# Rotary keys of the paged cache gathered straight into SBUF by GpSimd, instead of through a DRAM copy and ScalarE's loads

## What is computed

```python
# page_table (8, 32) int32: physical page of each of the 32 pages of a decode row
# cache_mla_latent (pages, 128, 256), cache_mla_krope (pages, 128, 32)
c_all  = concat([cache_mla_latent[page_table].reshape(b, 4096, 256), c], axis=1)
kr_all = concat([cache_mla_krope[page_table].reshape(b, 4096, 32), kr], axis=1)
s = (einsum('bqhc,bsc->bhqs', q_lat, c_all) + einsum('bqhr,bsr->bhqs', q_pe, kr_all)) * MLA_SCALE
p = masked_softmax(s)
o_lat = einsum('bhqs,bsc->bqhc', p, c_all)
```

## Time and profile before

| | |
|---|---|
| three runs | 736.41, 732.91, 735.43 us, median 735.43 |
| the profiled execution | 736.41 us, its span 734.6 us |
| tensor engine (PE) busy | 687.2 us, 94% |
| VectorE (DVE) / ScalarE (ACT) / GpSimd (POOL) busy | 439.2 / 212.3 / 64.2 us |
| moved by DMA | 178.60 MB, mean 243 GB/s |

### The profile page before, as it was taken

The page is one execution under the profiler, slowest core; times in us unless marked ns, Lnnn a source line. Parts: engine busy times, 40 slices in busy tenths (PEclk is TensorE's granted clock), DMA queues, the critical chain, the costliest instruction groups (busy, mean ns, idle before and its releaser), DMA issues.

```text
span 734.6 us, 14345 instructions
## 1 busy us (share of the span) xinstructions
PE 687.2 (94%) x5297; PEld 441.2 (60%) x5297; DVE 439.2 (60%) x1231; ACT 212.3 (29%) x579; POOL 64.2 (9%) x68
## 2 busy tenths in 40 slices
PE   9997999999979988789999999969999999999996
PEld 3443444544446655466776666547778888885452
DVE  3296799568647765675565555443577666644244
ACT  0302215545324443343334443221111111110111
POOL 0343341030000000202102000000000000000000
PEclk9999999989989999999999999999999999999999
DMA  9999994987879999996776788995110303026011
GB/s 342 412 415 421 417 397 174 369 306 311 307 214 339 355 375 326 378 364 232 233 247 219 264 288 251 328 366 234 58 57 1 115 1 115 1 103 271 29 50 39
DMA packets 64736, 178.60 MB, mean 243 GB/s; under 512 B 7225, under 2 KB 15698, under 8 KB 57370
## 3 DMA queue, kind: packets, MB, share of 16 engines
q1 hardware_dynamic: 47640, 124.88, 47.7%
q0 software_dynamic: 7840, 48.38, 16.6%
q10 hardware_dynamic: 9186, 4.42, 2.5%
HBM read 169.12 MB, written 12.72 MB: 248 GB/s over the span
## 4 chain that ended last, share of the span: by engine, by line
PE 67%; DMA 15%; SPq 6%; DVE 5%; issue 4%; ACT 2%; ACTq 0%; DVEq 0%
PE bank L1423 18%; PE bank L855 8%; PE bank L1463 8%; PE bank L1266 6%; DMA ring<-latent 6%; DMA W<-w_attn 4%; SPq L627 4%; PE bank L1018 3%; PE bank L1153 3%; PE bank L1250 3%; DMA projP<-x 2%; PE bank L1235 2%; PE bank L1132 2%; PE bank L1455 2%; PE bank L1140 2%
## 5 line engine op out<-in xcount | busy, mean ns | idle before, releaser
L855 PE MATMUL bank<-W,XG 128*128 128x494 f32 x192 | 85.2, 589 | 4.4 <-DMA W<-w_attn 3.9
L1484 ACT ACTIVATE projP<-bank 128x128 f32<-128x128 f32 (+5 forms) x87 | 33.6, 391 | 96.2 <-PE bank L1423 47.5
L2452 DVE TENSOR_TENSOR projP<-projP,bank 128x260 f32<-128x260 f32 x83 | 33.9, 423 | 45.1 <-PE bank L1423 44.3
L855 PEld LDWEIGHTS bank<-W,XG 128*128 128x128 f32 x192 | 35.8, 195 | 41.3 <-issue 40.0
L1266 PE MATMUL bank<-W 128*128 128x260 f32 x256 | 60.4, 389 | 0.0
L1484 ACT ACTIVATE W<-bank 128x512 f32<-128x512 f32 (+2 forms) x69 | 39.8, 582 | 66.6 <-PE bank L898 18.9
L1682 ACT ACTIVATE projP<-bank,projP 128x128 f32<-128x128 f32 (+3 forms) x96 | 49.8, 524 | 29.6 <-DVE projP L2154 29.1
L1266 PEld LDWEIGHTS bank<-W 128*128 128x128 f32 x256 | 47.3, 190 | 10.4 <-issue 3.2
L2154 DVE CUSTOM_DVE_ANT_0 bank<-bank,maskb 128x128 f32<-128x128 f32 (+3 forms) x96 | 45.8, 510 | 12.7 <-PE bank L1132 12.0
L1463 PE MATMUL bank<-ring,W 128*128 128x512 f32 x112 | 49.6, 594 | 1.4 <-issue 1.4
L1132 PE MATMUL bank<-W 64*128 64x128 f32 (+7 forms) x192 | 46.8, 471 | 1.0 <-ACT projP L1682 0.6
(11 more groups left out here) (436 smaller groups left out, 1119.8 us busy)
## 6 DMA issues: line engine op xcount, KB each, us to landing
ring<-latent SPq DMA_DIRECT2D x200, 256.0 KB, 6.7
XG<-latent SPq DMA_DIRECT2D x56, 256.0 KB
W<-w_gate SPq DMA_DIRECT2D x12, 1024.0 KB, 4.8
W<-w_attn SPq DMA_DIRECT2D x16, 494.0 KB, 9.9
rope_pages<-ring SPq DMA_DIRECT2D x2, 2048.0 KB, 10.3
KRR<-rope_pages ACTq DMA_DIRECT2D x32, 128.0 KB
ring<-w_out SPq DMA_DIRECT2D x2, 2048.0 KB, 13.2
o_win<-win SPq DMA_DIRECT2D x1, 4088.0 KB
```

Source lines behind the costliest of these rows:

```text
L855: mm = pe.matmul(bank[2 * (u % 2) + n][:, 0:GW], XG[:, k * TOK + tl * P:k * TOK + (tl + 1) * P], w_part(half, k, n), start=(k == 0), stop= ...
L1484: return act.activation(dst, src, ACT.Copy, scale=scale)
```

## The change

The changed kernel does without `rope_pages`, the two 2 MB gathers, the two stores and ScalarE's 32 loads. GpSimd gathers the rows of each pair straight from `krT` into `KRR`, by four gathers of 128 rows of 512 bytes (64 KB). Their row numbers are 64 more columns of `idxi`, made from a third copy of the page table (`pt4`) by four more small matmuls and one more VectorE instruction at the start, with a new table `exp4` of 128 columns among the first constants. The gathers of pair 0 stand behind GpSimd's memsets and wait for `pooled`; those of pair p wait for `ds` of pair p - 1. The 16 gathers of the selected branch (slc), which were the end of GpSimd's list, now stand between them, four each behind the gathers of pairs 7 to 10. SP's `o_win` and latent jobs no longer wait for `rope_out`. Two shared semaphores (`cst_in`, `x_again`) are split by what their waiters need.

```diff
+    put("exp4", (np.arange(4)[:, None] == p[None] // 32).astype(np.float32))
...
-            for half in range(2):
-                sp.wait_ge(S["rope_in"], 16 * (half + 1))
-                sp.dma_start(rope_pages.rearrange("(p h) n -> p h n", h=2)[:, half], slot[0]).then_inc(S["rope_out"], 16)
...
-            sp.wait_ge(S["rope_out"], 32)
             for m in range(3):
                 latents(m)
...
-            pool.wait_ge(S["pt_in"], 64)
-            pool.wait_ge(S["summed"], N_GATHERS)
-            gather(slot[0], rope_cache, pti[:, 320:321], S["rope_in"])
-            pool.wait_ge(S["rope_out"], 16)
-            gather(slot[0], rope_cache, pti[:, 321:322], S["rope_in"])
...
-            pool.wait_ge(S["idxs"], 1)
-            for r in range(4):
-                n = J_SLC + r
-                slot_free(pool, n)
+            pool.wait_ge(S["pooled"], 8)
+            mla = [c for c in chunks if c["kind"] == "mla"]
+            for p2 in range(16):
+                if p2:
+                    pool.wait_ge(S["ds"], mla[p2 - 1]["q"] + 1)
                 for j in range(4):
-                    gather(job(n)[:, j * 1024:(j + 1) * 1024], t["slc"], idxi[:, 32 + 4 * r + j:33 + 4 * r + j], S[slot_sem(n)])
+                    gather(KRR[:, j * P:(j + 1) * P], t["krT"], 32 + 4 * p2 + j, S["kr_landed"])
+                if 7 <= p2 < 11:
+                    n = J_SLC + p2 - 7
+                    pool.wait_ge(S["idxs"], 1)
+                    slot_free(pool, n)
+                    for j in range(4):
+                        gather(job(n)[:, j * 1024:(j + 1) * 1024], t["slc"], 96 + 4 * (p2 - 7) + j, S[slot_sem(n)])
...
+                for i2 in range(2):
+                    for jl in range(2):
+                        mm = pe.matmul(bank[7][64 * i2:64 * i2 + 64, 32:96].rearrange("p (a h l) -> p l a h", h=2, l=2)[:, jl], C("exp4", 64 * jl, 64, rows=4),
+                                       ptf[0:4, 32:96].rearrange("p (a i h) -> p i a h", i=2, h=2)[:, i2], start=True, stop=True)
...
-                    pe.wait_ge(S["kr_landed"], 32 * (p2 + 1))
+                    pe.wait_ge(S["kr_landed"], 64 * (p2 + 1))
...
-            rope_rows(0)
             act.wait_ge(S["prep_dve"], 1)
...
-                    c = SOFT_at[d]
-                    dec_exp(c)
-                    if c["kind"] == "mla" and c["no"] < 15:
-                        rope_rows(c["no"] + 1)
+                    dec_exp(SOFT_at[d])
...
+            ts(idxi[:, 32:96], bank[7][:, 32:96], 32.0, ALU.mult, C("mod", 1, 1), ALU.add).then_inc(S["idx"], 1)
```

More of the change, by code:

```diff
@@ L198, in build @@
         maskb = sb("maskb", SEQ, BF16)
-        idxi = sb("idxi", 32 + 16, I32)
-        pti = sb("pti", 32 + 32 + 256 + 2, I32)
+        idxi = sb("idxi", 32 + 64 + 16, I32)
+        pti = sb("pti", 32 + 64 + 32 + 256, I32)
         sm = sb("sm", SMALL)
-        rope_cache = t["krT"].rearrange("(a d) c -> a (d c)", d=ROPE_D)
-        rope_pages = nc.dram_tensor("rope_pages", (2 * P, 32 * P), F32, kind="Internal").ap()
         bank = [ctx.enter_context(nc.psum_tensor(f"bank{i}", [P, 512], F32)) for i in range(8)]
@@ L692, in _ @@
             slot_free(sp, J_X)
-            sp.dma_start(job(J_X).rearrange("p (t c) -> p t c", t=TILES), t["x"][0:SEQ].rearrange("(t p) c -> p t c", p=P)).then_inc(S["x_again"], 16)
+            sp.dma_start(job(J_X).rearrange("p (t c) -> p t c", t=TILES), t["x"][0:SEQ].rearrange("(t p) c -> p t c", p=P)).then_inc(S["xend_in"], 16)
             sp.wait_ge(S["z_ps"], z_at[tile_no["pa", 7], 1])
-            sp.dma_start(OA[0:DEC, 0:D_MODEL], t["x"][SEQ:TOK]).then_inc(S["x_again"], 16)
-            sp.dma_start(OB[:, 0:D_MODEL], t["norm_post"].broadcast_to([P, D_MODEL])).then_inc(S["x_again"], 16)
+            sp.dma_start(OA[0:DEC, 0:D_MODEL], t["x"][SEQ:TOK]).then_inc(S["xend_in"], 16)
+            sp.dma_start(OB[:, 0:D_MODEL], t["norm_post"].broadcast_to([P, D_MODEL])).then_inc(S["xend_in"], 16)
             for i, tl in enumerate(WO):
@@ L713, in _, with gather @@
             pool.dma_start(petile[0:CMP_BLOCK], t["pe"]).then_inc(S["pe_in"], 16)
-            def gather(dst, src, rows, sem):
+            def gather(dst, src, col, sem):
                 pool.indirect_dma_start(out=dst, out_offset=None, in_=src,
-                                        in_offset=bass.IndirectOffsetOnAxis(ap=rows, axis=0)).then_inc(sem, 16)
-            pool.wait_ge(S["idx"], 1)
+                                        in_offset=bass.IndirectOffsetOnAxis(ap=idxi[:, col:col + 1], axis=0)).then_inc(sem, 16)
+            pool.wait_ge(S["idx"], 2)
             pool.wait_ge(S["w_in7"], 16)
@@ L725, in _ @@
                     pool.wait_ge(S["summed"], g - N_HALVES + 1)
-                gather(half_slot(g), t["cmp"], idxi[:, g:g + 1], S[f"half{g % N_HALVES}"])
-            pool.wait_ge(S["pt_in"], 64)
-            pool.wait_ge(S["summed"], N_GATHERS)
-            gather(slot[0], rope_cache, pti[:, 320:321], S["rope_in"])
-            pool.wait_ge(S["rope_out"], 16)
-            gather(slot[0], rope_cache, pti[:, 321:322], S["rope_in"])
+                gather(half_slot(g), t["cmp"], g, S[f"half{g % N_HALVES}"])
             tiles_evicted(pool, 8)
@@ L818, in pages @@
                 pe.wait_ge(S["cst_first"], 16)
-                pe.wait_ge(S["ptf"], 2)
-                pe.matmul(bank[7][:, 0:32], C("exp8", rows=8), ptf[0:8, 0:32], start=True, stop=True).then_inc(S["prep_ps"], 1)
+                pe.wait_ge(S["ptf"], 3)
+                pe.matmul(bank[7][:, 0:32], C("exp8", rows=8), ptf[0:8, 0:32], start=True, stop=True)
+                for i2 in range(2):
+                    for jl in range(2):
+                        mm = pe.matmul(bank[7][64 * i2:64 * i2 + 64, 32:96].rearrange("p (a h l) -> p l a h", h=2, l=2)[:, jl], C("exp4", 64 * jl, 64, rows=4),
+                                       ptf[0:4, 32:96].rearrange("p (a i h) -> p i a h", i=2, h=2)[:, i2], start=True, stop=True)
+                mm.then_inc(S["prep_ps"], 1)
                 pe.wait_ge(S["pe_in"], 16)
@@ L1622, in _ @@
             copy(VV[:, :].rearrange("p (t c) -> p t c", t=TILES), pP[:, :, C_VS:C_KC]).then_inc(S["prep_by_act"], 1)
-            mla = [c for c in chunks if c["kind"] == "mla"]
-            def rope_rows(p2):
-                if p2:
-                    act.wait_ge(S["ds"], mla[p2 - 1]["q"] + 1)
-                else:
-                    act.wait_ge(S["pooled"], 8)
-                    act.wait_ge(S["rope_out"], 32)
-                for i2 in range(2):
-                    src = rope_pages[16 * p2 + 8 * i2:16 * p2 + 8 * i2 + 8].rearrange("(j q) (d c) -> (q d) j c", q=2, d=32)
-                    act.dma_start(KRR[64 * i2:64 * i2 + 64, 0:512].rearrange("p (j c) -> p j c", j=4), src).then_inc(S["kr_landed"], 16)
             for i, h in enumerate(HQ):
@@ L2143, in _ @@
             dve.wait_ge(S["prep_ps"], PREP_PS["idxs"])
-            ts(idxi[:, 32:48], bank[5][:, 16:32], C("mod", 2, 1), ALU.add).then_inc(S["idxs"], 1)
+            ts(idxi[:, 96:112], bank[5][:, 16:32], C("mod", 2, 1), ALU.add).then_inc(S["idxs"], 1)
             settle()
```

31 lines of the change are left out of this document (16 added, 15 removed).

## The result

In the measurement made beside the prediction the changed kernel took 752.1 us (749.96 to 753.76, four runs; three more executions on record took 751 to 757), the kernel before 734.2 us. The ratio is 1.027, with a 95% interval of 1.021 to 1.032: slower, by 18 us, where the forecast was 7 us faster. The forecast's upper end, 735.0, is missed by 17 us.

A forecast was written before the change was run, and what follows sets the result against it. It took the tensor engine (94% of the span) as the bound, with transfers bounding the attention from latents(4) to 300 us. -5.0 - 2.0 + 0.3 = -6.7 us, from the median 735.43, gave 728.7 us; range 725.0 to 735.0.

The forecast's parts named there:

- The wait of 5.0 us: At the first pair, the tensor engine's wait for KRR, 204.29 to 209.33 us, goes: -5.0 us.
- the clock's 2.0: At the first pair, without the wait, work from 209.33 to 214.85 us runs at the full clock: -2.0 us.
- the prediction's 186 to 208: Time in us when the last KRR row of pair 0 is there, 208 being the far end.
- So the stretch ends 7 us earlier.: Transfer-bound stretch to 300 us: latents(4) goes out 7.0 us earlier, so its end moves by 7 us and the gain stays.
- -6.7 us: Sum of the forecast over the whole kernel: -5.0 - 2.0 + 0.3 us.
- The bytes are equal: KRR of pairs 1 to 15, four GpSimd gathers for two ScalarE issues: 0 us, bounds 0 and +1 per pair.
- The round trip at no gain: Gathering and storing the pages ahead of the attention, now dropped: the sum gave its bytes no term.
- Landing 9.7 to 10.5 us after `ds`: Pairs 1 to 15: KRR is all there 9.7 to 10.5 us after the scores of the pair before.
- Rival C: Saturated stretch: KRR late by 0.5 us at five to nine pairs, beyond latent waits; 731 to 733 us, 13%.
- ScalarE's part: ScalarE without its 32 issues over the span: taken as 0, with -1.8 us as bound.
- Rival A: Attention pairs: KRR gathers land after 9.4 us under full DMA load, slower than before; 746 us, 9%.

The follow-up runs named there:

- later series: The changed kernel, not altered in anything, measured again on five other chips: 722.7, 721.7 and 722.4 us timed, 724.7 and 721.9 us in single runs.
- first series: The measurement of the changed kernel made beside the prediction, against the kernel before: 752.1 us, ratio 1.027.
- trip: Changed kernel, but only pair 0 gathered by GpSimd; pairs 1 to 15 come through stored pages and ScalarE's queue as before: 734.2 us, ratio 0.999.
- trip_unread: As trip, without ScalarE's 30 loads of KRR for pairs 1 to 15, whose KRR is left out of the computation: 724.3 us, ratio 0.985.
- none: Changed kernel without the KRR gathers of pairs 1 to 15; all pairs use the KRR of pair 0: 719.9 us, ratio 0.980.
- double: Changed kernel with four more gathers per pair for pairs 1 to 15, into places nobody reads, 60 gathers more: 729.1 us, ratio 0.993.
- c_after: The changed kernel, not altered in anything, measured again on another chip: 722.7 us, ratio 0.982.
- act: Changed kernel, but pairs 1 to 15 loaded straight from krT on ScalarE's queue, sixteen one-page loads per pair in place of four gathers: 857.9 us.
- four edits: Changed kernel with KRR elsewhere, a wait at SyncE's end, a GpSimd wait, or two KRR places gathered a pair earlier: 721.3, 721.0, 721.7, 722.9 us.

## Why the prediction was wrong, step by step

There are two misses. For the 722 us of the later series two steps failed, the gain at the first pair, which isn't kept, and the 0 us for the loads of the other pairs; the runs price both. For the 752.1 us of the first series no term of the sum accounts: the trace shows stalls beside GpSimd's gathers that the prediction has nowhere, and their cause stays open.

*The wait of 5.0 us and the clock's 2.0.* Right as steps: no wait, clock 1.00, and line 1250 7.6 us earlier in the first series; 5.4 us at line 1239 in trip, once the clock ahead of it is allowed for. KRR was there sooner than the prediction's 186 to 208: GpSimd's memsets came at 167.94, and its last gather of pair 0 was issued at 174.40, which with the worst landing of 19.8 us is 194. Over the whole execution the clock gives nothing back that shows: it is at the lower level for 24.6 and 14.4 us in the two traces of before and for 10.2 to 29.4 us in the five later ones of the changed kernel, four of which have it at 265 to 269 us instead.

*"So the stretch ends 7 us earlier."* This is the first step that failed in the sum. It treats a transfer-bound stretch as a block of fixed length that moves with its first job. But the time at which it ends is set by the bytes that remain and the rate, and between 200 and 275 us the DMA share was 0.97 and 1.02 in the two traces of before and 1.05 in trip. Trip has the forecast's early part, 5.4 us at the first pair; 3 to 4 us of it were gone at the sixth and nothing was left at the end. Of the -6.7 us, the runs leave -0.9, with an interval of 2.4 us to either side.

*"The bytes are equal", and so 0 us, for KRR of pairs 1 to 15.* This is the second. It is wrong by sign and size. The prediction bounded this term at 0 and +1 us per pair, from the landing alone, and never below zero, though it called the stretch transfer-bound and knew that the source was in rows of 512 bytes either way. The path of the packets differs, and trip_unread prices the old one at 10 us, while the gathers cost 2 to 7 (changed minus none, and double). The whole on later chips: -0.9 for the first pair, -10 for the loads, -4 for the round trip, +2 for the gathers, about -13; measured -12 to -13. These four are the steps of one chain of kernels from before to changed, so the sum has to come out and is no check of the parts; and each part holds for its place in that chain.

*The round trip at no gain.* The sum has no term for its 4 MB. The runs give it about 4 us with an interval of 6 to either side, from two chips, so this is the least certain part; trip_unread's late latents at the first pair speak for it, trip's trace, which has none, against it.

*Landing 9.7 to 10.5 us after `ds`.* About right: one wait for KRR per execution, of 2.0 to 2.5 us, in four of the five later traces. In c_after it ends at 464.28, 10.5 us after the scores of the pair before (453.40 + 0.40). Rival C had the mechanism, at five to nine pairs where there is one.

*ScalarE's part.* It is inside the 10 us, and small: the tensor engine's waits for ScalarE fell by 0.8 us from trip to trip_unread, those for latents by 8.5. The prediction's bound of 1.8 us holds. Each of the 30 issues held ScalarE 0.6 us, as in act.

*Rival A (746 us, gathers late).* Near the number of the first series and wrong by mechanism: that trace has no wait for KRR. What it has is stalls beside gathers that had no part in the forecast, on whichever engine waits for a semaphore. What is shown of this disturbance: it comes with GpSimd's gathers, in both kernels of that series and, but for single late records, in none of the later traces. What isn't: why, whether the gathers alone would do it there, and why the timed executions lost 10 us more than the traced one.

So both results lie outside 725 to 735, one 17 us above and one 2 to 3 us below, and for two different reasons: a term priced at zero that is worth -10 for the old loads and +2 to +7 for the new gathers, beside a gain of 7 that was given back; and a disturbance that no row ahead of the prediction shows, though the trace of before has it beside the slc gathers. That the later times come within 3 us of the range is partly luck: a gain that wasn't kept and one that wasn't foreseen have nearly the same size.

## What to carry to other kernels

Where transfers bound a stretch, ask what each queue's packets cost per MB, and not only how many bytes there are; freeing an engine at the head of such a stretch did little here but lengthen its waits in it. An engine's gain at one wait is worth what is left of it at the end of the next saturated stretch. And when a result contradicts the trace, run the unaltered kernel again beside the first experiment: here theories 1 and 2 and four edits went into a number that belonged to one series.

## What the runs showed of the hardware

- Loads of KRR in packets of 512 bytes slow the other queue: its packets of 2,048 bytes take 96 ns in the mean with them and 90 to 92 without (trip against trip_unread, and nine other traces), and the 16 engines move 337 against 366 GB/s at the same busy share of 1.02.
- The gathers of the same rows were recorded in packets of 4,096 bytes, and took 4.1% of the 16 engines per MB against 5.5. They left the other queue's packets at 90 to 91 ns.
- An issue on ScalarE's queue takes 0.6 us of ScalarE, with a page number from a register (16 take 9.7 us in act) or with a fixed address (trip). The page DMA: Bandwidth & Descriptors of the Trainium skill, section "SWDGE vs HWDGE vs iDMA", advises SyncE or ScalarE for plain transfers. Here sixteen such loads per pair in place of four gathers cost 136 us, by their issues.
- The rule that the prediction weighed, of the page SBUF — State Buffer of the Trainium skill, section "SBUF: two separate sides", that GpSimd's DMAs suffer beside VectorE, did not decide: between 200 and 275 us of a later trace a KRR gather took 0.95 us with VectorE busy for 72% of the time.
- In the first series, and in none of the five later ones with this kernel, the tensor engine stood beside 16 of the 19 groups of four gathers after 200 us, 24.2 us in all against 10.6, with semaphore updates late and records missing from the trace. The cause is open.
